# Three modulation vectors summed on TensorE at the ends of residual stages, one in the attention

## The chip, the cores and the metric

The kernel runs on one core of one Trainium2 chip. The metric is device time of one execution in microseconds (us), as the median of three runs. Beside it there is one profiled execution, whose instructions can be read one by one. TensorE is called PE here, its weight loads PEld, VectorE DVE, ScalarE ACT, GpSimd POOL and SyncE SP.

## What is computed

Two transformer blocks follow each other on 256 tokens of width 1024, everything in float32. The first block has two layers, each conditioned by a vector `c`: a small product of `silu(c)` with a wide matrix gives shift, scale and gate vectors of 1024 values each.

```python
cs = jax.nn.silu(c)
for l in range(2):
    if l == 1:
        kv_mod = cs @ kv_mod_w + kv_mod_b            # shift and scale for keys and values
        kv = shared_kv(x, kv_mod[:, :D], kv_mod[:, D:], kv_norm, w_kv)
    mod = cs @ mod_w[l] + mod_b[l]                   # six vectors of 1024
    sh_m, sc_m, g_m = mod[:, :D], mod[:, D:2*D], mod[:, 2*D:3*D]
    sh_f, sc_f, g_f = mod[:, 3*D:4*D], mod[:, 4*D:5*D], mod[:, 5*D:]
    h = modulate(rmsnorm(x, norm_mix[l]), sh_m, sc_m)
    mix = rglru_mixer(h, ...) if l == 0 else moba_mixer(h, ..., kv[0], kv[1], kv[2], rel_bias)
    x = x + g_m[:, None, :] * mix
    h = modulate(rmsnorm(x, norm_ffn[l]), sh_f, sc_f)
    x = x + g_f[:, None, :] * swiglu(h, ffn_w_gate[l], ffn_w_up[l], ffn_w_down[l])
```

These are fourteen modulation vectors: numbers 0 to 5 of layer 0, 6 to 11 of layer 1 (gate of the mixer 8, shift, scale and gate of the feed-forward part 9, 10 and 11), and 12 and 13 for keys and values. The second block is a mixture of a recurrence, a pooling and an attention, and then 16 experts. The change does not touch it.

## The kernel before

All weights are cut into 128x128 tiles, 16 tiles make a chunk of 1 MB, and the chunks lie in HBM in the order in which they are used. SP loads them one after the other into a ring of six slots (`weight_ring`), each load waiting until the chunk that last stood in the slot has been read. In the experts further slots join. The activations lie transposed, feature by token, 128 features a tile (`KD` = 8 tiles for the width 1024), so that a product column of 128 output features takes eight matmuls of 128x128 by 128x256. A float32 matmul shows in the trace as two MATMUL records.

There are two ways to make a modulation vector.

- **A group on TensorE** (`mod_group`, L485, listed in `GROUPS` as first column and width n). `silu(c)` stands as the stationary operand, 32 equal columns of it, and the weights are the moving one. In each of eight steps four matmuls write four strips of 32 rows of bank 6, each n·128 columns wide: a group of width 4 makes two vectors, one of width 2 makes one. ACT then copies bank 6 to SBUF (`mod_rows`, L1257), TensorE transposes the n pieces into bank 7 (`rows_to_columns`, L498), and DVE adds the bias (`mod_columns`, L1660).
- **A vector on DVE** (`mod_vectors`, L1672, listed in `VECTORS`). DVE takes four chunks out of the same ring and sums them in eight operations on 128x1024. TensorE then sums over the partitions with eight matmuls of one column (`add_partitions`, L508), and DVE adds the bias (`add_bias`, L1667).

Before, groups make vectors 0, 1, 2, 3, 4 and, in the attention, 8 and 9 together; DVE makes 5, 12, 13, 6, 7 and 10 beside the first feed-forward part and 11 beside the second. The sum over the partitions for number 10 stands in the attention (`if i == 2`).

The order of each engine is written out by hand. The stages that matter are: the recurrence of layer 0 and its output product; feed-forward 0 (22 columns each of gate and up, then `ffn_down0`); keys and values (`w_kv`, four key columns, then the values); queries; attention over 16 items (a head and a half of the tokens each); its output product (`attn_w_o`); feed-forward 1. A product that is added to the stream goes through `residual` (L538): column by column, DVE scales by the gate and adds, ACT squares (`squares`), TensorE sums the squares over the features with a matrix of ones (`sum_of_squares`). After the last column this becomes a chain through the engines: DVE adds, ACT squares, TensorE sums, ACT takes the root (`root`), DVE the reciprocal, DVE scales tile by tile (`normalise`), ACT shifts tile by tile (`shift`), and TensorE starts the next stage with the first tile.

## Time and profile before

| | us |
|---|---|
| median of three runs | 1777.69 (1777.51 to 1777.8) |
| the profiled execution | 1771.78 |
| its span, first to last instruction | 1770.0 |
| TensorE busy in it | 1534.1 (87%) |
| VectorE busy in it | 517.7 (29%) |
| ScalarE busy in it | 272.6 (15%) |
| mean clock granted to TensorE | 0.929 of full |

The profile page has the busy time of each engine, the span in 40 slices with TensorE's granted clock and the DMA rate, the DMA queues, the chain of work that ended last, and the costliest groups of instructions. Further views of the trace answer for a stretch: the instructions in order of time, busy time and clock by window, and the chain piece by piece. A busy matmul is not one at peak: the records of matmuls that follow each other overlap, so the pace is read from start to start.

### The profile page before, as it was taken

To read this page: it belongs to the slowest core of one execution; us is meant where nothing else is said; L and a number is where in the kernel's file an instruction comes from. 1 tells how busy PE (TensorE), PEld (TensorE's weight loads), DVE (VectorE), ACT (ScalarE), POOL (GpSimd) and SP (SyncE) were. 2 spreads that over 40 slices of the span, in tenths; PEclk is the share of its full clock that TensorE was granted. 3 is DMA by queue.
4 is the path that set the end of the run, shared out by engine and by line. 5 is a ranking of instruction groups with operands and counts; after the bars stand their busy time and mean duration, and the time that the engine had idled before them with its cause. 6 is when DMAs were issued, how large, how long until landed. Compare 5 with 4: busy or idle time off the path is not lost.

```text
span 1770.0 us, 25549 instructions
## 1 busy us (share of the span) xinstructions
PE 1534.1 (87%) x11252; PEld 1150.1 (65%) x11252; DVE 517.7 (29%) x1153; ACT 272.6 (15%) x666; POOL 66.8 (4%) x96
## 2 busy tenths in 40 slices
PE   7999999999999999999978889998988667666665
PEld 4787788887767888888766677786864323222222
DVE  3464444402043211006656454323321000000001
ACT  2241100002041000002323223131010000000001
POOL 0040000000000000000110110200000000000000
PEclk9999999999999999999999999999998877787877
DMA  9745678843463544343200001322769999999996
GB/s 400 295 163 194 255 310 313 314 182 119 153 228 139 223 153 151 143 143 119 96 25 2 26 26 49 119 107 84 319 260 420 419 419 420 420 420 420 420 420 288
DMA packets 57774, 405.93 MB, mean 229 GB/s; under 512 B 6200, under 2 KB 8504, under 8 KB 9152
## 3 DMA queue, kind: packets, MB, share of 16 engines
q1 hardware_dynamic: 53120, 384.06, 55.1%
q10 hardware_dynamic: 4544, 20.24, 2.9%
q8 instruction: 89, 1.46, 0.3%
q14 instruction: 21, 0.17, 0.0%
HBM read 403.21 MB, written 1.06 MB: 228 GB/s over the span
## 4 chain that ended last, share of the span: by engine, by line
PE 66%; DMA 24%; DVE 7%; ACT 2%; issue 1%; POOL 0%; SPq 0%; DVEq 0%; ACTq 0%; POOLq 0%
PE bank L476 65%; DMA arena<-weights 13%; DMA weight_ring<-weights 8%; DMA normed_T<-weights 3%; DVE arena L1652 3%; PE bank L483 1%; DVE arena L1658 1%; ACT arena L1255 1%; DVE arena L1655 1%; DVE ies_modulation_rows_rstd L1708 0%; DVE ies_modulation_rows_rstd L2045 0%; ACT ies_modulation_rows_rstd L1255 0%; ACT L1255 0%; DMA arena<-x 0%; POOL arena L2282 0%
## 5 line engine op out<-in xcount | busy, mean ns | idle before, releaser
L476 PE MATMUL bank<-normed_T,weight_ring 128*128 128x256 f32 x2640 | 608.9, 387 | 22.7 <-ACT arena L1255 9.6
L476 PEld LDWEIGHTS bank<-normed_T,weight_ring 128*128 128x128 f32 x2640 | 499.3, 192 | 109.1 <-ACT arena L1255 18.3
L476 PE MATMUL bank<-arena 64*64 64x64 f32 (+7 forms) x5350 | 412.0, 347 | 109.7 <-DMA arena<-weights 74.1
L476 PEld LDWEIGHTS bank<-arena 64*64 64x64 f32 (+5 forms) x5350 | 259.7, 147 | 264.1 <-DMA arena<-weights 110.4
L476 PE MATMUL bank<-arena,weight_ring 128*128 128x256 f32 x1456 | 329.9, 384 | 9.6 <-ACT arena L1255 3.6
L476 PEld LDWEIGHTS bank<-arena,weight_ring 128*128 128x128 f32 x1456 | 278.5, 193 | 50.2 <-issue 7.6
L1255 ACT ACTIVATE arena<-bank 128x256 f32<-128x256 f32 (+4 forms) x329 | 119.8, 372 | 1103.6 <-PE bank L476 745.5
L1658 DVE SCALAR_TENSOR_TENSOR arena<-arena,bank 128x256 f32<-128x256 f32 x141 | 59.4, 421 | 524.6 <-PE bank L476 268.3
L476 PE MATMUL bank<-weight_ring,arena 128*32 128x256 f32 (+1 forms) x896 | 84.9, 473 | 31.3 <-DMA weight_ring<-weights 28.2
L476 PEld LDWEIGHTS bank<-weight_ring,arena 128*32 128x32 f32 (+1 forms) x896 | 34.0, 130 | 76.0 <-DMA weight_ring<-weights 39.7
L1658 DVE SCALAR_TENSOR_TENSOR residual_T<-bank,modulation,residual_T 128x256 f32<-128x256 f32 x32 | 15.2, 483 | 198.4 <-PE bank L476 198.4
L483 PE MATMUL bank<-packed_consts,arena 128*128 128x128 f32 (+1 forms) x166 | 39.9, 339 | 36.3 <-DVE arena L1658 16.2
L2282 POOL TENSOR_TENSOR arena<-arena 128x512 f32<-128x512 f32 (+5 forms) x67 | 56.6, 851 | 330.0 <-DVE arena L1652 165.3
L483 PEld LDWEIGHTS bank<-packed_consts,arena 128*128 128x128 f32 (+1 forms) x166 | 22.5, 166 | 65.5 <-DVE arena L1658 28.3
L1658 DVE SCALAR_TENSOR_TENSOR arena<-weight_ring,silu_c,arena 128x1024 f32<-128x1024 f32 x49 | 62.8, 1282 | 1.0
L1255 ACT ACTIVATE normed_T<-residual_T 128x256 f32<-128x256 f32 x40 | 16.0, 414 | 227.2 <-DVE residual_T L1658 224.1
L1652 DVE TENSOR_TENSOR arena<-arena 128x256 f32<-128x256 f32 (+3 forms) x98 | 46.1, 482 | 16.0 <-ACT arena L1255 8.0
L1255 ACT ACTIVATE arena<-arena 128x256 f32<-128x256 f32 (+3 forms) x101 | 44.4, 464 | 29.0 <-DVE arena L1655 14.3
L1652 DVE TENSOR_TENSOR arena<-bank,arena 128x256 f32<-128x256 f32 (+2 forms) x97 | 32.4, 365 | 52.8 <-PE bank L476 52.3
L1652 DVE TENSOR_TENSOR arena<-arena,bank 128x512 f32<-128x512 f32 (+1 forms) x44 | 28.9, 661 | 50.7 <-PE bank L476 50.3
L2252 DVE COPY arena<-bank 128x256 f32<-128x256 f32 x16 | 6.8, 425 | 124.2 <-PE bank L476 124.2
L1658 DVE SCALAR_TENSOR_TENSOR arena<-arena 128x128 f32<-128x128 f32 (+4 forms) x97 | 35.4, 421 | 2.4 <-POOL arena L2282 2.0
(120 smaller groups left out, 527.5 us busy)
## 6 DMA issues: line engine op xcount, KB each, us to landing
weight_ring<-weights SPq DMA_DIRECT2D x240, 1024.0 KB, 6.3
arena<-weights SPq DMA_DIRECT2D x116, 1024.0 KB, 27.3
arena<-weights ACTq DMA_DIRECT2D x13, 1024.0 KB, 24.3
normed_T<-weights SPq DMA_DIRECT2D x8, 1024.0 KB, 28.6
arena<-packed ACTq DMA_DIRECT2D x1, 2720.0 KB
arena<-bias_by_distance ACTq DMA_DIRECT2D x2, 1024.0 KB, 17.6
arena<-x SPq DMA_DIRECT2D x1, 1024.0 KB, 5.1
normed_T<-weights ACTq DMA_DIRECT2D x1, 1024.0 KB, 4.7
```

What stands on the lines that cost most here:

```text
L476: return e.matmul(out, lhsT, rhs, start=start, stop=stop, skip_group_check=True)
L483: return e.transpose(out, in_, ident[0:n, 0:n])
L1255: return e.activation(out, in_, f, **kw)
L1652: return e.tensor_tensor(out, a, b, op)
L1655: return e.tensor_scalar(out, a, s1, s2, op0, op1) if s2 is not None else e.tensor_scalar(out, a, s1, None, op0)
L1658: return e.scalar_tensor_tensor(out=out, in0=a, scalar=sc, in1=b, op0=op0, op1=op1)
L2252: e.tensor_copy(m.ye, B[3][:, 0:QW]).then_inc(s.e_y, 1)
L2282: return e.tensor_tensor(out, a, b, op)
```

## The change

`GROUPS` gets the four vectors 8, 9, 10 and 11 as single groups of width 2, and `VECTORS` loses 10 and 11. Group 3 (vector 8) is summed after the last sum of squares of the recurrence's output product, group 4 (vector 9) after that of `ffn_down0`, group 6 (vector 11) after that of `attn_w_o`. Group 5 (vector 10) takes the place of the wide group in the attention. Their transposes stand in the second column of feed-forward 0 (group 3), between keys and values (group 4), at the end of the attention (5) and in the second column of feed-forward 1 (6). ACT's copies and DVE's bias additions move with them. `GROUP_COLS` is the list of counts that ACT waits for before it writes the row buffer again, since groups and vectors now alternate differently. The sum over the partitions for vector 7 now stands at the last column of feed-forward 0, and those for 10 and 11 are gone.

```diff
-GROUPS = ((0, 4), (16, 4), (32, 2), (64, 4))
-VECTORS = (5, 12, 13, 6, 7, 10, 11)
+GROUPS = ((0, 4), (16, 4), (32, 2), (64, 2), (72, 2), (80, 2), (88, 2))
+VECTORS = (5, 12, 13, 6, 7)
...
+GROUPS_BEFORE = 4
+GROUP_COLS = [i + 1 + len(VECTORS) * (i >= GROUPS_BEFORE) for i in range(len(GROUPS))]
...
+def vector_parts(f):
+
+    return share(f, KF - 2, len(VECTORS) * PER_VECTOR) if f < KF - 2 else int(f == KF - 1)
...
@@ def tensor_program(e, m, s, feed):
     sum_of_squares(NORM_FFN0, KD - 1)
+    steps(mod_group(3), KD)
...
-    early = mod_vectors(0, 1, 2, 3, 4, 5)
+    early = mod_vectors(*range(len(VECTORS)))

     def ffn0_fill(f):
-        steps(early, share(f, KF, 6 * PER_VECTOR))
+        if f == 1:
+            rows_to_columns(3)
+        steps(early, vector_parts(f))
...
     ffn(0, NORM_FFN0, KD, NORM_KV, ffn0_fill)
+    steps(mod_group(4), KD)
...
+    rows_to_columns(4)
     e.wait_ge(s.rel, REL["row"])
...
-    rows = mod_group(3)
+    rows = mod_group(5)
...
-        if i == 2:
-            steps(early, 1)
...
-    rows_to_columns(3)
+    rows_to_columns(5)
...
-    last = mod_vectors(6)
-    ffn(1, NORM_FFN1, 4 * KD, NORM_FINAL, lambda f: steps(last, f < PER_VECTOR or f == KD))
+    steps(mod_group(6), KD)
+    ffn(1, NORM_FFN1, 4 * KD, NORM_FINAL, lambda f: rows_to_columns(6) if f == 1 else None)
...
@@ def scalar_program(e, m, s, dram):
         if i:
-            e.wait_ge(s.mod_cols, i)
+            e.wait_ge(s.mod_cols, GROUP_COLS[i - 1])
...
+            if f == 0:
+                mod_rows((3, 6)[layer])
...
         act(m.KT[:, n, :], B[n][:, 0:T], ACT.Copy).then_inc(s.col_out, 1)
+    mod_rows(4)
...
-    mod_rows(3)
+    mod_rows(5)
...
@@ def vector_program(e, m, s, vectors):
-    ffn(0, NORM_FFN0, lambda f: steps(early, share(f, KF, 6 * PER_VECTOR)))
+    def ffn0_fill(f):
+        if f == 1:
+            mod_columns(3)
+        steps(early, vector_parts(f))
+    ffn(0, NORM_FFN0, ffn0_fill)
...
+    mod_columns(4)
     e.wait_ge(s.col, COL["v"] + 2)
...
-        if i == 2:
-            steps(early, 1)
-    mod_columns(3)
+    mod_columns(5)
...
-    last = mod_vectors(6)

     def weigh(f):
-        steps(last, f < PER_VECTOR or f == KD)
+        if f == 1:
+            mod_columns(6)
```

The order of instructions on TensorE shows three places. In these rows every matmul of the source is one, L476 and L483 of before are L484 and L491 after. The first place is the end of the recurrence's output product (rows with `arena,weight_ring`) and the start of feed-forward 0 (`normed_T,weight_ring`), before:

```order
40 L476 MATMUL bank<-arena,weight_ring 128x256 x10
41 L476 MATMUL bank<-normed_T,packed_consts 128x256
42 L476 MATMUL bank<-arena,weight_ring 128x256 x10
43 L476 MATMUL bank<-normed_T,packed_consts 128x256 x2
44 L476 MATMUL bank<-normed_T,weight_ring 128x256 x112
45 L476 MATMUL bank<-packed_consts,arena 128x1 x8
```

and after:

```order
42 L484 MATMUL bank<-arena,weight_ring 128x256 x10
43 L484 MATMUL bank<-normed_T,packed_consts 128x256 x2
44 L484 MATMUL bank<-weight_ring,_copies_modulation_rows_rstd 32x256 x32
45 L484 MATMUL bank<-normed_T,weight_ring 128x256 x32
46 L491 MATMUL bank<-packed_consts,_copies_modulation_rows_rstd 128x128 x2
47 L484 MATMUL bank<-normed_T,weight_ring 128x256 x80
```

Between the last sum of squares (x2) and the first matmul of feed-forward 0 there now stand the 32 matmuls of a group, and two transposes follow two columns later.

The second place is TensorE at the end of feed-forward 0, in keys and values (the matmuls of 512 columns are the values) and in the first items of the attention, before:

```order
69 L476 MATMUL bank<-normed_T,packed_consts 128x256 x2
70 L476 MATMUL bank<-arena,weight_ring 128x256 x32
71 L476 MATMUL bank<-weight_ring,arena 128x512 x16
72 L476 MATMUL bank<-normed_T,weight_ring 128x256 x64
73 L476 MATMUL bank<-arena 128x128
74 L476 MATMUL bank<-arena 128x256
75 L476 MATMUL bank<-arena 128x128
76 L476 MATMUL bank<-arena 128x256
77 L476 MATMUL bank<-packed_consts,arena 128x1 x8
78 L483 MATMUL bank<-packed_consts,arena 128x128
```

and after:

```order
72 L484 MATMUL bank<-normed_T,packed_consts 128x256 x2
73 L484 MATMUL bank<-weight_ring,_copies_modulation_rows_rstd 32x256 x32
74 L484 MATMUL bank<-arena,weight_ring 128x256 x32
75 L491 MATMUL bank<-packed_consts,_copies_modulation_rows_rstd 128x128 x2
76 L484 MATMUL bank<-weight_ring,arena 128x512 x16
77 L484 MATMUL bank<-normed_T,weight_ring 128x256 x64
78 L484 MATMUL bank<-arena 128x128
79 L484 MATMUL bank<-arena 128x256
80 L484 MATMUL bank<-arena 128x128
81 L484 MATMUL bank<-arena 128x256
82 L491 MATMUL bank<-packed_consts,arena 128x128
```

A group has come in ahead of the keys, two transposes between keys and values, and the eight matmuls of one column have left the attention.

The third place is the attention's steady part on TensorE, where one step of the group stands in every second item, before:

```order
84 L476 MATMUL bank<-arena 128x128 x2
85 L476 MATMUL bank<-weight_ring,_copies_modulation_rows_rstd 32x512 x4
86 L476 MATMUL bank<-arena 128x128
87 L483 MATMUL bank<-packed_consts,arena 128x128 x2
```

and after:

```order
88 L484 MATMUL bank<-arena 128x128 x2
89 L484 MATMUL bank<-weight_ring,_copies_modulation_rows_rstd 32x256 x4
90 L484 MATMUL bank<-arena 128x128
91 L491 MATMUL bank<-packed_consts,arena 128x128 x2
```

The step keeps its place and moves half the columns.

## Rows read from the trace of the kernel before

**Rows 1.** Profile page: DMA rate in 40 slices of 44 us, and the last chain.

```profile
GB/s 400 295 163 194 255 310 313 314 182 119 153 228 139 223 153 151 143 143 119 96 25 2 26 26 49 119 107 84 319 260 420 419 419 420 420 420 420 420 420 288
...
PE 66%; DMA 24%; DVE 7%; ACT 2%; issue 1%; POOL 0%; SPq 0%; DVEq 0%; ACTq 0%; POOLq 0%
```

**Rows 2.** Chain by time before feed-forward 0: start us, length us, what.

```profile
176.41 0.71 PE bank L476 x2
...
180.68 243.02 PE bank L476 x1150
```

**Rows 3.** TensorE in order of time, starts of keys and feed-forward 1: start, length, instructions [idle before].

```profile
428.98 16.66 PE L476 MATMUL bank<-arena,weight_ring 128*128 128x256 f32 x64 [3.57 <-ACT arena L1255]
...
555.39 5.03 PE L476 MATMUL bank<-normed_T,weight_ring 128*128 128x256 f32 x11 [3.57 <-ACT normed_T L1255]
```

**Rows 4.** Windows of 1 us: PE, PEld, DVE, ACT, POOL busy, PE clock, DMA share, GB/s.

```profile
130.00:131.00 1.00, 1.00 (x24) 0.61 (x20) 0.00 (x0) 0.34 (x1) 0.62 (x1) 1.00 0.85 131
133.00:134.00 1.00, 0.00 (x0) 0.00 (x0) 0.92 (x2) 1.00 (x4) 0.00 (x0) 0.94 1.05 434
178.00:179.00 1.00, 0.00 (x0) 0.00 (x0) 1.00 (x1) 0.00 (x0) 0.00 (x0) 0.63 0.00 0
185.00:186.00 1.00, 1.00 (x6) 0.82 (x5) 0.00 (x0) 0.00 (x0) 0.00 (x0) 0.96 0.00 0
427.00:428.00 1.00, 0.00 (x0) 0.00 (x0) 0.96 (x2) 0.00 (x0) 0.00 (x0) 0.72 0.00 0
434.00:435.00 1.00, 1.00 (x6) 0.83 (x5) 0.56 (x2) 1.00 (x3) 0.00 (x0) 0.87 0.00 0
553.00:554.00 1.00, 0.00 (x0) 0.00 (x0) 1.00 (x1) 0.00 (x0) 0.00 (x0) 0.86 0.00 0
560.00:561.00 1.00, 1.00 (x4) 0.83 (x4) 0.00 (x0) 0.00 (x0) 0.00 (x0) 0.72 0.00 0
```

**Rows 5.** TensorE by time: group 2, the one group of width 2.

```profile
127.99 3.66 PE L476 MATMUL bank<-weight_ring,ies_modulation_rows_rstd 128*32 128x256 f32 x64
```

**Rows 6.** TensorE by time in the attention: group steps (128x512), their neighbours, last transposes.

```profile
499.13 1.07 PE L476 MATMUL bank<-weight_ring,ies_modulation_rows_rstd 128*32 128x512 f32 x8
500.13 0.49 PE L476 MATMUL bank<-arena 128*128 128x128 f32 x2
...
502.43 1.06 PE L476 MATMUL bank<-weight_ring,ies_modulation_rows_rstd 128*32 128x512 f32 x8
...
519.22 0.66 PE L483 MATMUL bank<-packed_consts,ies_modulation_rows_rstd 128*128 128x128 f32 x4 [0.74 <-ACT ies_modulation_rows_rstd L1255]
```

**Rows 7.** VectorE by time in the attention: its first items, then one of the steady part.

```profile
490.10 0.29 DVE L1655 TENSOR_SCALAR arena<-arena 128x128 f32<-128x128 f32 x1
491.49 0.17 DVE L1652 TENSOR_TENSOR modulation<-bank,packed_consts 128x8 f32<-128x8 f32 x1 [1.10 <-PE bank L476]
491.57 0.41 DVE L1658 SCALAR_TENSOR_TENSOR arena<-bank,arena 128x256 f32<-128x256 f32 x1
...
500.66 0.29 DVE L1658 SCALAR_TENSOR_TENSOR arena<-bank,arena 128x128 f32<-128x128 f32 x1 [0.65 <-PE bank L476]
```

**Rows 8.** All engines by time, feed-forward 1: the sum over partitions for vector 11.

```profile
620.17 1.84 PE L476 MATMUL bank<-packed_consts,arena 128*128 128x1 f32 x16
...
621.88 8.45 PE L476 MATMUL bank<-normed_T,weight_ring 128*128 128x256 f32 x38
```

**Rows 9.** TensorE by time: two transposes of group 2 inside the recurrence's output product.

```profile
155.08 0.38 PE L483 MATMUL bank<-packed_consts,ies_modulation_rows_rstd 128*128 128x128 f32 x2
155.30 4.50 PE L476 MATMUL bank<-arena,weight_ring 128*128 128x256 f32 x20
```

**Rows 10.** By time: TensorE's first values; ScalarE's shifts for the keys, last key copy.

```profile
445.48 1.02 PE L476 MATMUL bank<-weight_ring,arena 128*128 128x512 f32 x2
...
428.33 3.30 ACT L1255 ACTIVATE arena<-arena,modulation 128x256 f32<-128x256 f32 x8 [2.41 <-DVE arena L1658]
...
445.68 0.38 ACT L1255 ACTIVATE arena<-bank 128x256 f32<-128x256 f32 x1 [3.07 <-PE bank L476]
```

More of the change, by code:

```diff
@@ L1814, in ffn @@
         residual(m.mods(layer, 5))
-    early = mod_vectors(0, 1, 2, 3, 4, 5)
-    ffn(0, NORM_FFN0, lambda f: steps(early, share(f, KF, 6 * PER_VECTOR)))
+    early = mod_vectors(*range(len(VECTORS)))
+    def ffn0_fill(f):
[3 more added lines that the diff above has]
+    ffn(0, NORM_FFN0, ffn0_fill)
     scaled_gain(m.mod[:, 96 + KD:112], "kv_norm")
```

## Prediction

> **What bounds the kernel now.** I read the page first, then the chain piece by piece over the first 800 us, then each engine in order of time and windows of 1 us where the chain leaves TensorE. The last chain is TensorE for 66% and DMA for 24% [rows 1]. The DMA part belongs to the experts at the end, where the rate stands at 420 GB/s. Ahead of them the rate falls to 2 to 26 GB/s for some slices, so the load queue stands still there with its slots full, and the experts' loads start when TensorE and the others free space. What is saved in the first block is therefore saved at the end.
>
> In the first block the chain is nearly all TensorE. It leaves it at the ends of the residual stages. The last sum of squares starts at 176.41; then ACT's root, DVE's reciprocal and the first tile of DVE and ACT follow, and feed-forward 0 starts at 180.68 [rows 2]. The same hole of 3.57 us idle stands ahead of the keys at 428.98 and of feed-forward 1 at 555.39 [rows 3].
>
> Each hole costs a second time, through TensorE's clock [rows 4]. A window's clock is a mean of the two levels, 1.00 (2.4 GHz) and 0.50 (1.2 GHz), so 0.63 in window 178 means that it fell at 178.26. By window 185 it was back at 185.08. Likewise it fell at 427.44 and rose at 434.26, and fell at 553.72 and rose at 560.56: three slow spells of 6.8 us. TensorE worked in them from 180.68, 428.98 and 555.39 on, for 4.40, 5.28 and 5.17 us at half speed, and lost half of that: 2.20 + 2.64 + 2.58 = 7.4 us.
>
> **Part 1: groups in the holes.** Group 2 has the same 32 matmuls (64 records) as each new group and took 3.66 us, 127.99 to 131.65 [rows 5]. A sum of squares is two records of 256 columns, and 38 such records from 621.88 on take 8.45 us, 0.22 each [rows 8]. So the group can start at 176.41 + 0.44 = 176.85 and ends its last record by 180.5; the next stage can't start before 180.68. The hole hides it with 0.2 us to spare, the other holes alike, being as long. Nothing is added, and if the group were slower, only the excess over 0.2 would be paid.
>
> What it gives back is the clock. In group 2 the clock stood at 1.00, at 130 to 131 too, two us into the group, and fell only at 133.88 (0.94 in window 133), 2.2 us after it had ended [rows 4, 5]. So such a group counts as work. With it the hole has two idle pieces of a microsecond or less instead of 3.57 us. I take the whole 7.4 us as saved; the bounds are 0 (the clock falls all the same) and 7.4. The first column of the next stage, now at full speed, still finds its tiles: ACT shifts eight in 3.30 us, 0.41 each [rows 10], a tile takes 0.44.
>
> The group's pace rests on four strips running at once: 64 records in 3.66 us against 64 x 0.22 = 14.1 one after the other, a factor of 3.8 [rows 5, 8]. The Trainium skill, page TensorE: Matmul & The Clock Gate, Part 3 (Packing small matmuls), measured 2.38 times for three column tiles. By its ratio, carried on to four tiles as an estimate, the factor would be 3.2, a group would take 4.4 us, and three would stick out by 0.6 us each: the sum would be 1.8 us less. The trace has this very shape, and it decides.
>
> The weights: a group takes four chunks in 3.66 us. In the holes the DMA share is 0.00 in windows 178, 427 and 553 [rows 4], so all six slots were full and SP was waiting for a free one. Four full slots and two more are what the group and the first column need. A chunk of 1.05 MB at 434 GB/s (window 133) takes 2.4 us, so the four are back 10 us later, while TensorE and DVE take two chunks in a column of 6.9 us. SP's order is otherwise unchanged, and its DVE chunks are fewer.
>
> **Part 2: the attention.** A step of the wide group takes 500.13 - 499.13 = 1.00 us of TensorE, a step of width 2 takes 3.66/8 = 0.46 or a little less, start to start; I take 0.45. Two items take 502.43 - 499.13 = 3.30 us [rows 6], and in them DVE has one idle piece of 0.65 us, at 500.66, which waits for TensorE's product right behind the step [rows 7]. So the step is on the loop TensorE, DVE, TensorE, and DVE can follow a gain of 0.55 with 0.1 to spare: 8 x 0.55 = 4.4 us. The bounds are 0 and 4.5. In the first items DVE was ready at 490.10 + 0.29 = 490.39 for the next item, but waited for the column sums of vector 10 and started it at 491.57 [rows 7]: 1.2 us. At the end the copy and the transposes (0.66 for four against 0.38 for two [rows 6, 9]) are half as long: 0.5 with ACT's part of the 0.74 wait. Together 6.1 us.
>
> **Part 3: the column sums of vector 11** go from feed-forward 1: 621.88 - 620.17 = 1.7 us of a TensorE without idle time [rows 8]. DVE's eight large operations there and its share in feed-forward 0 go too; they lay beside TensorE and give nothing. Feed-forward 0 keeps five column sums.
>
> **Part 4: what is added.** Two transposes in feed-forward 0 and two in feed-forward 1, 0.2 us each from start to start [rows 9]: 0.4. ACT's copies for them stand behind the first tanh, and TensorE asks a column (6.9 us) later, so nobody waits. Between keys and values there is a new wait: the transposes need ACT's `mod_rows(4)`, which is queued behind the copy of the last key column. That copy starts at 445.68 and takes 0.38, the second one as much, so TensorE goes on at about 446.5 instead of 445.48, and two transposes take 0.3: +1.3 us [rows 10, 9]. Bounds: 0.2 (the transposes alone) and 2. Behind TensorE only the values wait, and DVE's `mod_columns(4)` is long done before it is needed.
>
> **Sum:** -7.4 - 6.1 - 1.7 + 0.4 + 1.3 = -13.5 us. The span of 1770.0 becomes 1756.5, the profiled time of 1771.78 about 1758.3. The median of the runs is 5.9 above the profiled time, and I carry that over: 1777.69 - 13.5 = 1764.2.
>
> **Rivals.**
>
> *The clock falls all the same.* The idle pieces left around the sum of squares might be enough. Then the group runs at full speed to 178.26 and its rest of 2.2 us at half, to 182.7, 2.0 behind 180.68; with a spell of 6.8 us as now, the stage then loses 1.2 more to 185.08: 3.2 against 2.2 now, 1 us more in each hole. Sum: -13.5 + 7.4 + 3 = -3.1, 1774.6. Against it speaks the clock through group 2. Chance 0.10. The Trainium skill, same page, Part 1, section on a second failure mode (psum-queue depth-cycling), says that frequent short idle pieces between groups of matmuls can make the clock swing; that is this rival. The steady attention, with idle pieces of 0.2 us per item pair, doesn't decide it.
>
> *The attention doesn't follow.* If DVE, with 0.1 us to spare, or ACT becomes its bound, the 4.4 shrinks to nothing and the sum is -9.1: 1768.6. The idle piece of 0.65 speaks against. Chance 0.11.
>
> *Swallowed before the end.* If the experts' stream of loads was tied to something that doesn't move, nothing is left: 1777.7. The slices of 2 to 26 GB/s speak against. Chance 0.05.
>
> *The ring runs dry, slower.* If a group found none of its four chunks loaded, it would take 4 x 2.4 = 9.7 us, 6.0 beyond the hole, three times, and the clock would fall as now: -13.5 + 18 + 7.4 = +11.9, 1789.6. Each chunk that is missing costs 2.4 us, and with two missing in each hole (3 x 4.8 = 14.4, less the 0.2 to spare) the gain of 13.5 is gone: that is the point from which it decides. DMA at rest in all three holes says that six stand ready. Chance 0.03.
>
> **How the numbers follow.** My forecast has 0.71. The predicted time is 1764.2. The range takes in the attention rival and the values' wait at 2 us, and on the lower side a slow spell at the start of the attention or in a later hole that may be missed when all moves by 13 us (each is worth up to 2.6 us): 1760 to 1770, with 0.82 of the chance. 0.2% (3.6 us) is about what a measurement of this kernel can tell from no change. Faster by more than that: forecast, attention rival and half of the clock rival, 0.71 + 0.11 + 0.05 = 0.87. Within: the other half of it and the swallowed gain, 0.10. Slower: 0.03.
>
> **What would show it.** In the trace of after, 32-column matmuls of 256 columns stand in the three holes with an idle piece of about 0.2 us behind them, and the windows there have a clock of 1.00; the first 64 records of keys take 14 us, not 16.5. Two items of attention take about 2.75 us. TensorE idles about 0.9 us ahead of the transposes between keys and values. From the start of feed-forward 1 to its end it is 4 us shorter. I am wrong if the clock row shows 0.50 behind the holes, if a DMA wait stands ahead of a group, or if an item pair stays at 3.3 us.

## The result and the profile after

| us | before | after |
|---|---|---|
| median | 1777.74 (1777.51 to 1784.73, 4 runs) | 1759.6 (1757.09 to 1762.15, 4 runs) |
| profiled execution, its span | 1771.78, 1770.0 | 1759.8, 1758.0 |
| TensorE / VectorE busy | 1534.1 / 517.7 | 1529.4 / 498.8 |
| mean granted clock | 0.929 | 0.936 |

The ratio is 0.9889, with a 95% interval from 0.9861 to 0.9917. The forecast was 1764.2, with a range from 1760 to 1770. The direction and the changed stages came out as said, but the time fell 4.6 us further, to just below the range.

The three holes are the first place. TensorE of after in order of time (start, length, instructions, idle time before and who ended it) answers [rows 2, 3]:

```profile
179.11 0.70 PE L484 MATMUL bank<-normed_T,packed_consts 128*128 128x256 f32 x2 [0.59 <-ACT normed_T L1266]
179.74 3.66 PE L484 MATMUL bank<-weight_ring,ies_modulation_rows_rstd 128*32 128x256 f32 x64
183.38 14.05 PE L484 MATMUL bank<-normed_T,weight_ring 128*128 128x256 f32 x64
...
426.09 3.66 PE L484 MATMUL bank<-weight_ring,ies_modulation_rows_rstd 128*32 128x256 f32 x64
429.74 14.05 PE L484 MATMUL bank<-arena,weight_ring 128*128 128x256 f32 x64
444.54 0.44 PE L491 MATMUL bank<-packed_consts,ies_modulation_rows_rstd 128*128 128x128 f32 x2 [0.75 <-ACT ies_modulation_rows_rstd L1266]
444.81 2.74 PE L484 MATMUL bank<-weight_ring,arena 128*128 128x512 f32 x6
...
546.38 3.66 PE L484 MATMUL bank<-weight_ring,ies_modulation_rows_rstd 128*32 128x256 f32 x64
550.02 2.18 PE L484 MATMUL bank<-normed_T,weight_ring 128*128 128x256 f32 x9
```

From the start of the last sum of squares to the next stage is 183.38 - 179.11 = 4.27 us, as it was before (180.68 - 176.41). The group fills the hole and pushes nothing. The first 64 records of keys take 14.05 us where they took 16.66. The windows say why. Their columns are those of [rows 4], of which PEclk (the third from the end) counts here:

```profile
178.00:179.00 1.00, 0.51 (x3) 0.11 (x1) 0.56 (x2) 0.36 (x1) 0.00 (x0) 1.00 1.06 451
185.00:186.00 1.00, 1.00 (x6) 0.90 (x5) 0.47 (x2) 1.00 (x3) 0.00 (x0) 1.00 1.01 295
427.00:428.00 1.00, 1.00 (x24) 0.63 (x20) 1.00 (x1) 0.00 (x0) 0.00 (x0) 1.00 0.00 0
434.00:435.00 1.00, 1.00 (x7) 0.87 (x6) 1.00 (x4) 1.00 (x4) 0.00 (x0) 1.00 0.99 418
548.00:549.00 1.00, 1.00 (x25) 0.57 (x21) 0.96 (x2) 0.00 (x0) 0.00 (x0) 1.00 0.61 82
553.00:554.00 1.00, 1.00 (x7) 0.87 (x6) 0.00 (x0) 0.99 (x2) 0.00 (x0) 1.00 1.04 442
```

The clock is 1.00 (2.4 GHz) in and behind the holes, where [rows 4] had 0.63 to 0.96; it falls nowhere from 143 to 490 us or from 500 to 780 us. No DMA wait stands ahead of these groups.

In the attention the step is half as wide, as [rows 6] showed it before:

```profile
497.02 0.64 PE L484 MATMUL bank<-weight_ring,ies_modulation_rows_rstd 128*32 128x256 f32 x8
497.59 0.49 PE L484 MATMUL bank<-arena 128*128 128x128 f32 x2
...
499.18 0.33 PE L491 MATMUL bank<-packed_consts,arena 128*128 128x128 f32 x1 [0.22 <-DVE arena L1669]
...
499.89 0.64 PE L484 MATMUL bank<-weight_ring,ies_modulation_rows_rstd 128*32 128x256 f32 x8
...
512.90 0.64 PE L484 MATMUL bank<-weight_ring,ies_modulation_rows_rstd 128*32 128x256 f32 x8
514.07 0.44 PE L491 MATMUL bank<-packed_consts,ies_modulation_rows_rstd 128*128 128x128 f32 x2 [0.53 <-ACT ies_modulation_rows_rstd L1266]
```

Two items take 499.89 - 497.02 = 2.87 us instead of 3.30. The step takes 0.57 from start to start (1.00 before), and not the 0.45 it takes in a row of its kind.

### The profile page after: what moved, and what is told of

It reads as the page before. It is cut to its first block, busy times and chain, and to the rows that moved or that the text cites. A ratio compares the mean times of both kernels' runs of the same rounds, so it can differ in the third digit from the quotient of the medians.

```text
span 1758.0 us, 25855 instructions
## 1 busy us (share of the span) xinstructions
PE 1529.4 (87%) x11416; PEld 1146.6 (65%) x11416; DVE 498.8 (28%) x1138; ACT 272.8 (16%) x669; POOL 66.6 (4%) x96
## 4 chain that ended last, share of the span: by engine, by line
PE 66%; DMA 24%; DVE 6%; ACT 2%; issue 1%; SPq 0%; POOL 0%; DVEq 0%; ACTq 0%; POOLq 0%
PE bank L484 65%; DMA arena<-weights 13%; DMA weight_ring<-weights 7%; DMA normed_T<-weights 3%; DVE arena L1666 3%; PE bank L491 1%; DVE arena L1672 1%; ACT arena L1266 1%; DVE arena L1669 1%; SPq L2391 0%; DVE ies_modulation_rows_rstd L2063 0%; ACT L1266 0%; DMA arena<-x 0%; POOL arena L2300 0%; ACT ies_modulation_rows_rstd L1266 0%
## 5 line engine op out<-in xcount | busy, mean ns | idle before, releaser
L484 PE MATMUL bank<-normed_T,weight_ring 128*128 128x256 f32 x2640 | 606.9, 386 | 15.6 <-ACT arena L1266 9.6
L484 PEld LDWEIGHTS bank<-normed_T,weight_ring 128*128 128x128 f32 x2640 | 498.3, 192 | 101.4 <-ACT arena L1266 18.2
L484 PE MATMUL bank<-arena 64*64 64x64 f32 (+7 forms) x5350 | 409.4, 345 | 111.3 <-DMA arena<-weights 75.6
L484 PEld LDWEIGHTS bank<-arena 64*64 64x64 f32 (+5 forms) x5350 | 257.6, 145 | 262.5 <-DMA arena<-weights 116.5
L484 PE MATMUL bank<-arena,weight_ring 128*128 128x256 f32 x1456 | 326.1, 381 | 6.1 <-DVE arena L1672 3.1
L484 PEld LDWEIGHTS bank<-arena,weight_ring 128*128 128x128 f32 x1456 | 275.9, 191 | 45.5 <-DVE arena L1666 4.3
L484 PE MATMUL bank<-weight_ring,arena 128*32 128x256 f32 (+1 forms) x896 | 85.0, 472 | 32.7 <-DMA weight_ring<-weights 29.6
L484 PEld LDWEIGHTS bank<-weight_ring,arena 128*32 128x32 f32 (+1 forms) x896 | 34.0, 129 | 76.7 <-DMA weight_ring<-weights 40.6
L491 PE MATMUL bank<-packed_consts,arena 128*128 128x128 f32 (+1 forms) x166 | 39.3, 334 | 36.5 <-DVE arena L1672 16.2
L491 PEld LDWEIGHTS bank<-packed_consts,arena 128*128 128x128 f32 (+1 forms) x166 | 22.0, 162 | 64.8 <-DVE arena L1672 27.4
L1672 DVE SCALAR_TENSOR_TENSOR arena<-weight_ring,silu_c,arena 128x1024 f32<-128x1024 f32 x35 | 44.9, 1282 | 0.7
L484 PE MATMUL bank<-weight_ring,ies_modulation_rows_rstd 128*32 128x256 f32 (+1 forms) x448 | 38.3, 464 | 4.9 <-DMA weight_ring<-weights 4.8
```

Source lines behind the costliest of these rows:

```text
L484: return e.matmul(out, lhsT, rhs, start=start, stop=stop, skip_group_check=True)
L491: return e.transpose(out, in_, ident[0:n, 0:n])
L1672: return e.scalar_tensor_tensor(out=out, in0=a, scalar=sc, in1=b, op0=op0, op1=op1)
```

## Where the time went: three traces of each

The kernel before ran again in every comparison that follows: in 75 of its executions on four chips the time went from 1770.71 to 1785.48, with a median of 1776.6. Their mean clock went from 0.936 to 0.918, and the longer times mostly go with a lower clock, though not one by one (0.931 at 1770.71, 0.932 at 1779.09). Ten executions of after went from 1757.09 to 1762.15. A "spell" is a stretch in which the granted clock stands at 0.50. One trace of each is therefore little to go by, and I took three, cut at the same instructions: holes 1 to 3 are the 4.27 us each; "recurrence 2" goes from the first matmul of the second block's recurrence to its last 64x64 one, and is the same code in these two kernels. The row of feed-forward 1 ends, in each trace, at the same sum of squares, three output columns ahead of its last one; from there to the last sum is 32.3 us in all of them.

| us | before, three traces | after, three traces |
|---|---|---|
| feed-forward 0 | 244.0, 243.4, 243.5 | 242.1, 242.1, 242.1 |
| keys up to the values | 16.5, 16.2, 16.2 | 15.1, 15.1, 15.1 |
| attention | 32.2, 33.5, 33.5 | 27.5, 26.0, 26.0 |
| feed-forward 1 | 206.4, 205.6, 205.6 | 202.3, 202.3, 202.3 |
| **section**, hole 1 to feed-forward 1 | 585.4, 584.8, 585.0 | 573.2, 571.7, 571.7 |
| recurrence 2 | 276.9, 283.9, 277.4 | 274.8, 276.7, 279.8 |
| span | 1770.0, 1774.5, 1770.8 | 1758.0, 1755.3, 1756.1 |

On average the section is 585.1 - 572.2 = 12.9 us shorter (forecast 13.5), recurrence 2 2.3, and the span 1771.8 - 1756.5 = 15.3. So the gain in the first block reaches the end of the program. The medians of all executions lie some 17 apart, and these traces of before are on the fast side of its scatter.

## The experiments

### Both kernels once more, on other chips

> The kernel before, unchanged, for a second trace of it. The section that the change touches (last sum of squares ahead of feed-forward 0 to that behind feed-forward 1) took 617.7 us in the first trace. If the 5.9 us between the profiled 1771.78 and the median 1777.7 lie in slow spells of TensorE's clock in unchanged code, this section is again 617 to 619 us, and the first 180 us and the part behind 794 us hold the rest. If they lie in the touched section, it is 620 us or more.

1775.76 us (1771.73 to 1785.0), ratio 1.0003 [0.9979, 1.0026]. So two measurements of the same kernel agree within 0.3%, though single executions lie 13 us apart. The trace taken here ran 4.6 us longer than the first one, and not in the section that the change touches (584.8 us for 585.4): recurrence 2 took 7.0 more and the part ahead of hole 1 1.8 more, with the clock's spells elsewhere, and the part behind recurrence 2 3.6 less.

> The changed kernel, unchanged, for ten more times and a second trace. My sum says 13.5 us below before (1776.3 on this chip, so 1762.8); the first measurement said 18 (1758.3). The stretch from the last sum of squares ahead of feed-forward 0 to the end of feed-forward 1 should again be 12 us shorter than before's. If the median lies near 1763, the surplus was scatter of the runs; if near 1758 again, something outside that stretch gained too.

1760.04 us (1757.1 to 1761.64), ratio 0.9911 [0.9879, 0.9943] on that chip, where before had 1774.11. The attention took 26.0 us: the first trace of after had a slow spell in it, at 491 to 494, which cost 1.5.

### The clock alone

```diff
+    def warm(n):
+        e.wait_ge(s.mod, mods_done[0])
+        for _ in range(n):
+            mm(B[7][:, 0:T], m.ones, m.pk[:, 0:T], True, True)
...
     sum_of_squares(NORM_FFN0, KD - 1)
+    warm(8)
...
     ffn(0, NORM_FFN0, KD, NORM_KV, ffn0_fill)
+    warm(8)
...
+    warm(8)
     last = mod_vectors(6)
```

It is the kernel before with eight matmuls of constants in each hole, whose products nobody reads.

> The kernel before with eight matmuls of constants in each of the three holes (3.5 us of TensorE work whose result nobody reads), and no vector moved. If the gain in the holes is the clock: no slow spell behind them, 7.4 us faster in the touched section (617.7 becomes 610.3). If the clock has nothing to do with it and the gain came from work taken off the engines: no change, 0 us.

TensorE ahead of the keys:

```profile
423.39 0.70 PE L476 MATMUL bank<-normed_T,packed_consts 128*128 128x256 f32 x2 [0.59 <-ACT normed_T L1263]
423.92 3.62 PE L476 MATMUL bank<-packed_consts 128*128 128x256 f32 x16
427.66 14.05 PE L476 MATMUL bank<-arena,weight_ring 128*128 128x256 f32 x64
```

The keys take 14.05 us with no group at all: it is the idle time of the hole that costs the clock, and matmuls of constants keep it as well as a group does. The section took 579.3, 5.8 less than the mean of before. That is the clock's term by itself, with an attention 0.4 longer than that mean (33.5). Against the first trace of before, the three stages behind the holes are 7.3 us shorter, which is the forecast term. Against the mean it isn't 7.4, because the spells behind the holes are 3.4 us long in some executions and 6.8 in others: in the second trace of before TensorE worked 3.0 + 4.6 + 3.2 us in them, a loss of 5.4. The time, 1776.25 (1766.26 to 1779.37), ratio 0.9978 [0.9952, 1.0003], shows less than the section: four of ten executions lie at 1766 to 1770 and six at 1776 to 1779. By the total alone this kernel can't be told from before; the clock's term is read from the section.

One hole alone (of the three `warm(8)` only the middle one stays):

> The kernel before with eight matmuls of constants in the hole ahead of the keys alone (their products are read by nobody). If the clock's fall behind a hole is made by that hole's idle time, the first 64 records of keys take 13.9 us instead of 16.2 to 16.5, and the other two holes keep their spells: the section is 2.3 to 2.6 us below 584.8 to 585.4. If the clock's fall is made by more than one hole's idle time, the other holes' spells change too. For the recurrence of the second block: as for the kernel before, 277 to 284 us by either theory unless the clock falls at another instant.

```profile
181.00:182.00 1.00, 0.43 (x1) 0.46 (x2) 1.00 (x4) 1.00 (x3) 0.00 (x0) 0.54 0.00 0
427.00:428.00 1.00, 1.00 (x7) 0.87 (x6) 0.96 (x2) 0.00 (x0) 0.00 (x0) 1.00 0.00 0
434.00:435.00 1.00, 1.00 (x6) 0.90 (x5) 0.71 (x2) 1.00 (x4) 0.00 (x0) 1.00 1.07 131
549.00:550.00 1.00, 0.00 (x0) 0.00 (x0) 1.00 (x1) 0.00 (x0) 0.00 (x0) 0.86 0.00 0
```

The filled hole keeps 1.00 and the other two fall (0.54, 0.86): each hole makes its own spell. From the first key product to the first value is 13.89 us, as in the kernel with all three filled. The section took 580.7, 4.4 less, because this attention had no spell either: 30.98 us. I take it below for before's attention without a disturbance; it is one trace of a kernel that differs from before in the filled hole alone. The one execution took 1779.02 all the same, with 287.1 in recurrence 2.

### The groups as work in the way

```diff
     sum_of_squares(NORM_FFN0, KD - 1)
-    steps(mod_group(3), KD)
...
+        if f == 0:
+            steps(mod_group(3), KD)
+        if f == 2:
             rows_to_columns(3)
```

Groups 4 and 6 move alike, behind the second key column and behind the first column of feed-forward 1.

> The changed kernel with the three groups taken out of the holes and put behind the first column of each feed-forward part and behind the second column of the keys, where TensorE has no idle time. The clock theory: the slow spells are back (7.4 us), and each group costs its 3.65 us: 18 us slower than the changed kernel in the touched section (605.5 becomes about 623.8), about as slow as before or 6 us slower. Without the clock: 11 us slower than the changed kernel.

```profile
181.66 8.62 PE L484 MATMUL bank<-normed_T,weight_ring 128*128 128x256 f32 x32 [3.57 <-ACT normed_T L1267]
190.21 3.66 PE L484 MATMUL bank<-weight_ring,ies_modulation_rows_rstd 128*32 128x256 f32 x64
```

The hole of 3.57 is back, and the group's 3.66 us with it. Feed-forward 0 took 248.4 (+6.3), the keys 20.3 (+5.2), feed-forward 1 208.7 (+6.4). The section is 589.6, 17.4 more than after's, and the time 1775.47 (1773.47 to 1777.84), no better than before's. A place in a hole is worth 5 to 6 us against the same work elsewhere: the group's 3.66 us and most of what the spell costs that an empty hole leaves behind. The forecast of the clock theory was 18 us, that without the clock 11.

### The attention alone

```diff
-GROUPS = ((0, 4), (16, 4), (32, 2), (64, 4))
-VECTORS = (5, 12, 13, 6, 7, 10, 11)
+GROUPS = ((0, 4), (16, 4), (32, 2), (64, 2))
+VECTORS = (5, 12, 13, 6, 7, 9, 10, 11)
...
-        steps(early, share(f, KF, 6 * PER_VECTOR))
+        steps(early, share(f, KF, 7 * PER_VECTOR + 1))
...
-        if i == 2:
-            steps(early, 1)
```

Vector 9 is made by VectorE too, and the column sums of vector 10 stand in feed-forward 0.

> The kernel before with the attention's part alone: the group there is of width 2, the column sums of vector 10 stand in feed-forward 0, and vector 9 is summed on VectorE there too, so that feed-forward 0 gets two more column sums, 3.4 us. The attention from its first product to the output product took 32.2 us before and 27.5 after. If it stands on its own, it is again 27.5 us, and the whole is 1.3 us faster than before; by the size that I forecast (6.1 us) it would be 26.1 us and the whole 2.7 us faster. If the shorter attention hangs on the holes, it stays at 30 us or more.

The attention took 26.0 us, as in after, so this gain doesn't hang on the groups in the holes. But the kernel took 1780.7 us (1777.91 to 1782.6), ratio 1.0024 [1.0009, 1.0039]. The end of feed-forward 0:

```profile
348.71 1.89 PE L476 MATMUL bank<-normed_T,weight_ring 128*128 128x256 f32 x8
353.71 3.30 PE L476 MATMUL bank<-packed_consts,arena 128*128 128x1 f32 x16 [3.10 <-DVE arena L1656]
```

The last column sums waited 3.1 us for VectorE, and the clock fell behind it, at 354 to 361. Feed-forward 0 took 255.4 us. The next kernel tells whether it is VectorE's load or the spacing:

```diff
-        steps(early, share(f, KF, 7 * PER_VECTOR + 1))
+        steps(early, share(f, KF - 2, 7 * PER_VECTOR) if f < KF - 2 else int(f == KF - 1))
```

> The kernel with the attention's part of the change alone, but VectorE's parts in feed-forward 0 put in its first 20 columns with the last column sum at the 21st, as the changed kernel has them, where the earlier one had them up to the last column and TensorE waited 3.1 us for VectorE at its end. If that wait was the spacing's fault, feed-forward 0 takes about 247 us instead of 255.4, and the attention 26.0 as there: the section is some 3 us below before's 585.4, 582. If VectorE is short of time with seven vectors beside feed-forward 0 however they are spaced, feed-forward 0 stays above 250, and the time stays at or above that of before.

It was the spacing: feed-forward 0 took 248.7 us, the section 581.9, and the time is 1772.01 (1770.14 to 1779.13), ratio 0.9968 [0.995, 0.9986]. Part of what is above the 247 expected is one wait for a load:

```profile
217.52 3.69 PE L476 MATMUL bank<-normed_T,weight_ring 128*128 128x256 f32 x16 [1.30 <-DMA weight_ring<-weights]
```
Here VectorE's parts had to end a column ahead of the last sum.

### The step in the attention

```diff
-    rows = mod_group(5)
+    steps(mod_group(5), KD)
     scores(0)
...
-            if i % 2 == 0:
-                steps(rows, 1)
```

> The changed kernel with the eight steps of group 5 taken out of the attention and put right ahead of it, where they cost 3.65 us of TensorE. In the changed kernel two items take 2.87 us, and a step 0.57 of them. If TensorE's order still sets the pace, two items take 2.30 us. If VectorE (2.65 us of work in two items) has become the bound, they take 2.65 us and the attention falls by 8 x 0.22 = 1.8 us only, so that the whole is 1.9 us slower than the changed kernel.

Queries and values took 3.0 us more and the attention 3.0 less (23.0): nothing gained, 1757.54 in one execution. Two items take 501.27 - 498.71 = 2.56 us and TensorE waits 0.44 for VectorE in each pair:

```profile
498.44 0.44 PE L491 MATMUL bank<-packed_consts,arena 128*128 128x128 f32 x2 [0.44 <-DVE arena L1667]
498.71 0.82 PE L484 MATMUL bank<-arena 128*128 128x128 f32 x4
...
500.99 0.44 PE L491 MATMUL bank<-packed_consts,arena 128*128 128x128 f32 x2 [0.44 <-DVE arena L1667]
501.27 0.82 PE L484 MATMUL bank<-arena 128*128 128x128 f32 x4
```

VectorE has no idle piece in these items; the same operation starts 2.56 us later in the next pair:

```profile
499.61 0.41 DVE L1670 SCALAR_TENSOR_TENSOR arena<-bank,arena 128x256 f32<-128x256 f32 x1
502.17 0.42 DVE L1670 SCALAR_TENSOR_TENSOR arena<-bank,arena 128x256 f32<-128x256 f32 x1
```

So VectorE's limit is 2.56 us a pair, and after's 2.87 is still 0.3 above it. The rival "the attention doesn't follow" is out for this width, and would come in at the next step down: 0.57 us less of TensorE gave only 0.31.

### Transposes behind the values, and further idle pieces filled

```diff
-    rows_to_columns(4)
     e.wait_ge(s.rel, REL["row"])
...
+    rows_to_columns(4)
     for n in range(HEADS):
```

> The changed kernel with the two transposes of group 4 behind the values, not between keys and values. The wait for ScalarE's copy (0.75 us, and the pipeline that runs dry) should go and the transposes cost 0.2 us: from the first key product to the first query product 1.0 us less. If the wait only moves behind the values, nothing is gained.

Keys up to the values took 13.9 us instead of 15.1, what follows 0.2 more (42.2 for 42.0): the new wait and its transposes cost 1.19 us, and 0.97 of that can be had back. One execution took 1756.69.

With this, and matmuls of constants in further idle pieces (between the steps of group 0, ahead of the recurrences, in the second and third item of the attention; nobody reads their products):

```diff
...
     steps(mod_group(2), KD)
+    warm(7)
...
+        if i in (2, 3):
+            warm(1)
...
     ffn(1, NORM_FFN1, 4 * KD, NORM_FINAL, lambda f: rows_to_columns(6) if f == 1 else None)
+    warm(8)
```

> The changed kernel with the transposes later and with matmuls of constants, whose results nobody reads, in the idle pieces that are left: beside the first group, behind group 2, in the second and third item of the attention and behind feed-forward 1. Those are the places of the slow clock spells that the trace of the changed kernel still has up to 800 us (23 to 37, 139 to 143, 490 to 495, 787 to 795 us: 27 us of spells, 22 with TensorE at work, so 11 us lost). The clock theory: most of these go, 7 to 11 us faster than the changed kernel besides the 1.0 of the transposes. If filling an idle piece only helped where real work lay in it: no change.

1751.6 us (1750.27 to 1753.65), ratio 0.9861 [0.9825, 0.9896], mean clock 0.943 in its trace, where the clock falls for the first time at 892 us. And on another chip:

> The kernel with the group 4's transposes behind the values and matmuls of constants (read by nobody) in the idle pieces, once more, beside the changed kernel on this chip: it took 1751.6 us where the changed kernel took 1760.0. If that difference is the kernel's, it is again 6 to 10 us below the changed kernel; if it was a lucky set of executions, less than 4.

1751.61 (1750.76 to 1751.79), ratio 0.9858 [0.9826, 0.989]; one execution of after there took 1757.92. This version beats both kernels, after by 6 to 8 us, of which 1 is the transposes'. What each filled piece is worth by itself was not measured. More of the same:

```diff
+        if ct:
+            for _ in range(7):
+                mm(B[3][:, 0:T], m.ones, m.pk[:, 0:T], True, True)
         e.wait_ge(s.prepared, 2 * ct + 2)
```

> The kernel with matmuls of constants in the idle pieces (whose products nobody reads), with more of them: four in the idle piece of 2.02 us in the second block's recurrence (about 860), and seven ahead of each of two idle pieces of 3.35 us (about 953 and 1015), where the trace still has spells of 6.8 us at half clock at 946 to 954 and 1008 to 1015. If the clock falls there only because TensorE idles, both spells go and the time falls by 3 to 7 us, to 1745 to 1749. If the added matmuls stand in the way of the work behind them (TensorE waits for VectorE there), the recurrence gets longer and the time stays at 1751 to 1753.

Besides these, four matmuls stand in an idle piece of 2.02 us at about 851. It took 1759.57 (1754.33 to 1763.0), ratio 0.9893 [0.9867, 0.9918]. The trace of TensorE around the added matmuls, first without them (the kernel above), then with:

```profile
943.34 0.70 PE L484 MATMUL bank<-normed_T,weight_ring 128*128 128x256 f32 x2
947.38 1.11 PE L491 MATMUL bank<-packed_consts,arena 128*128 128x128 f32 x4 [3.35 <-DVE arena L1687]
...
957.02 1.75 PE L484 MATMUL bank<-arena 64*64 64x64 f32 x24 [1.35 <-DVE arena L1681]
960.60 0.68 PE L484 MATMUL bank<-arena 64*64 64x64 f32 x16 [1.84 <-DVE arena L1681]
```

```profile
947.05 3.19 PE L484 MATMUL bank<-packed_consts 128*128 128x256 f32 x14
950.57 0.66 PE L491 MATMUL bank<-packed_consts,arena 128*128 128x128 f32 x4 [0.33 <-DVE arena L1696]
...
958.79 1.75 PE L484 MATMUL bank<-arena 64*64 64x64 f32 x24 [2.85 <-DVE arena L1690]
962.38 0.68 PE L484 MATMUL bank<-arena 64*64 64x64 f32 x16 [1.84 <-DVE arena L1690]
```

The idle piece of 3.35 is filled and TensorE runs at full speed behind it, but VectorE is what this stretch waits for. TensorE now waits 2.85 us a little later instead of 1.35, with the 1.84 behind it as before, and then the clock falls: half clock at 964 to 978, 13.7 us over dense work, where it had been half at 947 to 954. Recurrence 2 took 280.4 us (273.0 and 274.6 without). That is one trace, of a stretch whose length varies by itself, as the next part shows; but the slowest of the eight executions without these matmuls (1753.65) is faster than the fastest with them (1754.33). So filling the holes gained where the work behind them was TensorE's, and here, ahead of a stretch that waits for VectorE, it lost. Which of the three added pieces cost how much was not measured.

### Vector 11, and the rest that is open

A surplus in the unchanged recurrence 2 remained. Vector 11's part of the change was done alone in the kernel before:

```diff
...
-    last = mod_vectors(6)
-    ffn(1, NORM_FFN1, 4 * KD, NORM_FINAL, lambda f: steps(last, f < PER_VECTOR or f == KD))
+    steps(mod_group(4), KD)
+    ffn(1, NORM_FFN1, 4 * KD, NORM_FINAL, lambda f: rows_to_columns(4) if f == 1 else None)
```

> The kernel before with one part of the change alone: vector 11 is summed by TensorE in the hole ahead of feed-forward 1 (group 4, two transposes in its second column), and no longer by VectorE beside feed-forward 1. The touched section, from the last sum of squares ahead of feed-forward 0 to feed-forward 1's last product, took 585.4 and 584.8 us in two traces of before; here feed-forward 1 should take 206.4 - 4.1 = 202.3 us and the rest stay, so 581 us. Theory A (the surplus of 4 to 5 us in the unchanged recurrence of the second block belongs to this part of the code): the time falls by 4.1 + 4 to 5, to 8 or 9 us below the runs of before, and the recurrence from its first matmul to its last 64x64 one takes 274 to 277 us. Theory B (it is only where the clock's spells fall): the time falls by 4.1, and the recurrence takes 277 to 284 us, with a spell about 72 us after its start.

and undone alone in the kernel after:

```diff
...
-    steps(mod_group(6), KD)
-    ffn(1, NORM_FFN1, 4 * KD, NORM_FINAL, lambda f: rows_to_columns(6) if f == 1 else None)
+    last = mod_vectors(5)
+    ffn(1, NORM_FFN1, 4 * KD, NORM_FINAL, lambda f: steps(last, f < PER_VECTOR or f == KD))
```

> The changed kernel with this one part undone: vector 11 is summed by VectorE beside feed-forward 1 again, with its eight column sums on TensorE, and the third hole is empty. Feed-forward 1 should take 206.4 us instead of 202.3, a loss of 4.1. Theory A (the surplus belongs to this part): 4 to 5 us more are lost, 8 or 9 us slower than the changed kernel (1760.0), 1768 to 1769, with the spell 72 us after the start of the second block's recurrence. Theory B (it doesn't): 1764, and that spell is as absent as in the changed kernel.

The first took 1772.1 us (1764.65 to 1778.43), ratio 0.9962 [0.9941, 0.9983], section 581.4, recurrence 2 280.6 with the spell at 72 us. The second took 1763.91 (1760.32 to 1767.23), ratio 0.9919 [0.9893, 0.9945], section 574.8, recurrence 2 276.9 without that spell. The first one's median lies 7.2 below that of before, between the two theories (4.1 and 8 or 9), so there the trace has to decide, with the long recurrence 2 of theory B; the second one is at theory B's 1764. So vector 11 is worth 3 to 4 us (feed-forward 1: 202.3 for 205.9, and 205.4 for 202.3), and the traces don't give it the surplus.

Both kernels unchanged, once more:

> The kernel before once more, for a third trace of it. Theory 'where the spells fall': the length of the second block's recurrence (from its first matmul to its last 64x64 one: 276.9 and 283.9 us in the two traces so far) goes with the instant at which the clock falls at its start: 280 to 284 us where it falls 0.3 to 0.5 us before the first matmul, 274 to 277 where it falls at another instant; and a third trace may show either. Theory 'it belongs to the kernel': it takes 277 us or more again, with a spell 72 us after its start, wherever the first fall stands.

> The changed kernel once more, for a third trace. Theory 'where the spells fall': if the clock falls 0.3 to 0.5 us before the first matmul of the second block's recurrence, that takes 280 us or more, as in the kernel before; at other instants 274 to 277. Theory 'it belongs to the kernel': 274 to 277 again, without a spell 72 us after its start, wherever the first fall stands. The section from the sum of squares ahead of feed-forward 0 to feed-forward 1's last product: 571.7, or 573.2 with a spell in the attention.

1772.59 and 1757.92 us, one execution each; their traces are the third ones of the table above.

The spell in question, 72 us after the first matmul of recurrence 2, in windows of before and of after at the same instructions (PEclk is the third number from the end):

```profile
871.00:872.00 1.00, 0.99 (x21) 1.00 (x23) 0.97 (x3) 0.00 (x0) 0.73 (x1) 0.58 0.48 147
872.00:873.00 1.00, 1.00 (x18) 0.88 (x15) 0.69 (x1) 0.47 (x2) 0.40 (x1) 0.50 0.95 401
```

```profile
862.00:863.00 1.00, 0.61 (x21) 0.64 (x23) 0.97 (x4) 0.00 (x0) 0.34 (x1) 1.00 0.29 49
863.00:864.00 1.00, 1.00 (x21) 0.84 (x17) 1.00 (x1) 0.77 (x2) 0.79 (x1) 1.00 0.91 360
```

What TensorE did before is alike in both: eight matmul records, an idle piece of 2.02 us, four records, 0.63 idle (0.64). All eight traces of kernels near before have this spell, none of the seven near after (the three kernels with filled pieces are left out; one of their traces has a spell at 68.5 us). The traces sorted by the first fall of the clock at the start of recurrence 2:

| clock falls, us from the first matmul | recurrence 2, us (traces near before in bold) |
|---|---|
| -1.8 to -1.6 | **279.4**, 274.7, 274.8 |
| -1.1 to -0.7 | 276.6, 276.7, 279.8, 276.9 |
| -0.5 to -0.2 | **280.6, 280.7, 283.9, 280.8, 277.4** |
| +0.3 to +0.9 | **287.1, 276.9**, 273.9 |

Neither theory holds as it was put. The third trace of after fell at -1.0 and took 279.8, where its kin at -1.0 took 276.7; so the first fall alone doesn't set the length, and "274 to 277 whatever happens" is wrong too. What stands is that the same code differs by up to 13 us through spells alone, that the traces near before average 280.8 and those near after 276.2, and that their first falls lie in different places. That the spells earlier in the program set where the later ones fall would explain this, but no run here shows it. It stays open.

## Why the prediction was right and where it failed

- **Holes' clock, -7.4.** The mechanism is shown by the rows of after, by the filled holes without groups (-5.8 for the section) and by the one filled hole. The size holds for the first trace of before; in the others it was about 2 us less, since spells were shorter.
- **The group hides in the hole.** Right, with less to spare than the 0.2 written: the sum of squares takes 0.63 us to the group's start, not 0.44, and 0.63 + 3.66 is the hole's 4.27 to within 0.02, so the idle piece forecast behind the group isn't there. The pace of [rows 5] came back exactly, 64 records in 3.66 us, three times. The ratio of 2.38 for three column tiles in the Trainium skill, page TensorE: Matmul & The Clock Gate, Part 3 (Packing small matmuls), would, carried on to four as an estimate, have made it 4.4 us, which the traces refute for this shape.
- **The ring runs dry, or the clock falls all the same.** Neither: no DMA wait ahead of a group in the holes, and 1.00 in the windows. Nor was the gain swallowed before the end: the spans are 15.3 us apart.
- **The attention, -6.1.** The total is near by chance: the first traces differ by 4.7, the means of three by 6.6. The two undisturbed attentions are 30.98 and 26.03, which is -4.95. The steps gave 8 x 0.43 = 3.4 and not 4.4, because a step of 0.57 us was put at 0.45, a price from a row of such steps without other work between them [rows 5]. The first items and the end gave the other 1.5. What made up for it is a spell of 3.4 us in before's attention, at 492 to 496, which the sum left out and which cost 1.3. In the first trace of after a spell of its own took 1.5 of it back.
- **Column sums of vector 11, -1.7, and transposes, +0.4.** With the clock's 2.6 they make up feed-forward 1's -4.1, measured -4.1 in the first traces.
- **The new wait, +1.3.** Measured 1.19, with 0.75 idle.
- **The step that failed** is the last line of the sum: "The median of the runs is 5.9 above the profiled time, and I carry that over". It took the time of all code outside the changed stages as fixed. The changed stages themselves came out at -12.9 for the forecast -13.5, but the median fell by 18.1 (1777.74 to 1759.6). The 5.9 was scatter between executions of before (1770.7 to 1785.5), which goes in the main with the clock's spells: its second trace, 4.6 us longer, had the extra time in unchanged code. After scatters by 5 and not by 15, and its profiled executions (1759.8, 1757.1, 1757.92) lie 0 to 3 us below its median. Recurrence 2, which isn't touched, was 2.3 us shorter in the three traces of each and 4.6 over all kernels near the two. Without the 5.9 the sum gives 1758.3 against 1759.6 measured, partly by luck, as it starts from an execution of before that lies 5 us below the median of all. The range had too little room below: 4.2 us, for one or two spells that may be missed. Why the unchanged code has fewer or cheaper spells in after stays open.

## What to carry to other kernels

In this kernel a dependency chain at a stage's end that leaves TensorE idle for 3.6 us costs twice, once as idle time and once as half speed in the stage behind it; real work of just that length is free there and worth 5 to 6 us against its place elsewhere, and even matmuls that nobody reads paid (5.8 us of the section), where what follows is bound by TensorE. Price a small operation by a row in which it stands among the work that it will stand among. Where a kernel's executions scatter, take several traces of before, and sum against the profiled execution or the median, but don't carry the difference of the two over as if it were fixed.

## What the runs showed of the hardware

- TensorE's granted clock isn't a function of the program: the same instructions with the same idle pieces ran at 1.00 in one trace and at 0.50 in another, and the spell behind the first hole of before took 6.8 us in one trace and 3.4 in two. The spells took 3.4, 6.8, 10.2 or 13.7 us, once 17.1 and once 20.5 (the last one of each trace aside). And 75 executions of one single-core program, on four chips, spread over 14.8 us with the mean clock from 0.936 to 0.918. An execution's time is read best beside its clock.
- Four strips of 32 columns at work together count as activity for the clock: each hole of before had a spell beginning in it or at its end, in all three traces, and with a group in it the clock stayed at 1.00, in all nine holes of the three traces of after. In group 0, whose steps have waits of up to 1.4 us for loads between them, a spell began at 21 to 23 us in the same three traces.
- A wait filled ahead of a stretch that VectorE bounds moved the wait and the clock's fall, here to denser work behind it. The kernel took 1759.6 us for 1751.6, on different chips; by the ratios to before (0.9893 for 0.9861 and 0.9858) it is 6 us, and their intervals overlap.
